# First MLP: four of twelve modulation chunks summed on TensorE in column groups

## What is computed

```python
c_act = jax.nn.silu(c)
for layer in range(DEPTH):
    mod = (c_act @ ada_w[layer] + ada_b[layer])[:, None, :]
    sh_a, sc_a, gt_a, sh_m, sc_m, gt_m = jnp.split(mod, 6, axis=-1)
    ...
    h = modulate(rms_norm(x, mlp_norm[layer]), sh_m, sc_m)
    x = x + gt_m * squared_relu_mlp(h, mlp_w1[layer], mlp_w2[layer])
    if layer == N_A_LAYERS - 1:
        kv_mod = (c_act @ kv_ada_w + kv_ada_b)[:, None, :]
```

## Time and profile before

| | us |
|---|---|
| median of 3 runs | 1641.82 |
| lowest, highest | 1637.86, 1643.93 |
| the profiled execution | 1641.37 |
| its span | 1639.5 |

### The profile page before, as it was taken

How to read it: one execution, slowest core, us unless ns; L and a number is a source line. 1 busy time by engine, 2 the same in 40 slices (tenths; PEclk the granted TensorE clock), 3 DMA queues, 4 the chain that set the end, 5 groups by cost and what they waited for, 6 DMA issues and landing times.

```text
span 1639.5 us, 21996 instructions
## 1 busy us (share of the span) xinstructions
PE 1425.1 (87%) x8482; PEld 1241.7 (76%) x8482; DVE 940.7 (57%) x1551; ACT 678.1 (41%) x1124; POOL 306.7 (19%) x257
## 2 busy tenths in 40 slices
PE   5779699999679799869999664879999898789999
PEld 1669598878679678659999554558999777579998
DVE  2777698886834554565444545446555555544443
ACT  2355444343512233334444334325444455344442
POOL 0633011010666950001001102001100100011110
PEclk9898899999778555579999776788999999889999
DMA  9877288997357220236665233027766435236651
GB/s 353 266 234 232 86 261 312 324 301 232 96 163 243 89 65 1 68 104 182 197 188 176 69 108 85 1 77 196 227 174 188 146 136 170 64 103 194 186 180 46
DMA packets 248791, 267.38 MB, mean 163 GB/s; under 512 B 10992, under 2 KB 182768, under 8 KB 248304
## 3 DMA queue, kind: packets, MB, share of 16 engines
q1 hardware_dynamic: 246064, 263.52, 51.7%
q10 hardware_dynamic: 2624, 2.47, 0.5%
HBM read 264.81 MB, written 1.15 MB: 162 GB/s over the span
## 4 chain that ended last, share of the span: by engine, by line
PE 71%; DVE 13%; issue 5%; ACT 5%; DMA 4%; POOL 1%; ACTq 0%; SPq 0%; DVEq 0%
PE bank L489 13%; PE bank L490 13%; PE bank L491 13%; PE ps_s L573 4%; PE ps_s L489 3%; PE ps_s L490 3%; PE ps_s L491 3%; PE ps_p L490 3%; PE ps_p L491 3%; PE ps_p L489 3%; DVE wlo L1103 2%; DVE acc L1122 2%; DMA wring<-in_mlp_w 2%; PE ps_p L586 2%; ACT whi L1984 2%
## 5 line engine op out<-in xcount | busy, mean ns | idle before, releaser
L1103 DVE TENSOR_TENSOR wlo<-wring,whi 128x1024 fp32r<-128x1024 f32 (+1 forms) x373 | 455.8, 1243 | 239.8 <-ACT whi L1984 235.8
L1984 ACT ACTIVATE whi<-wring 128x1024 fp32r<-128x1024 f32 (+1 forms) x373 | 388.5, 1051 | 382.3 <-PE ps_p L491 131.5
L489 PE MATMUL bank<-h_hi,whi 128*128 128x256 f32 x1216 | 352.8, 290 | 12.6 <-DVE h_lo L1197 11.2
L490 PE MATMUL bank<-h_lo,whi 128*128 128x256 f32 x1216 | 349.8, 288 | 0.0
L491 PE MATMUL bank<-h_hi,wlo 128*128 128x256 f32 x1216 | 349.3, 287 | 0.0
L489 PEld LDWEIGHTS bank<-h_hi,whi 128*128 128x128 f32 x1216 | 239.5, 197 | 18.1 <-DVE h_lo L1197 12.8
L490 PEld LDWEIGHTS bank<-h_lo,whi 128*128 128x128 f32 x1216 | 239.6, 197 | 0.7
L491 PEld LDWEIGHTS bank<-h_hi,wlo 128*128 128x128 f32 x1216 | 239.2, 197 | 0.0
L2394 POOL TENSOR_TENSOR ex<-ex 128x512 f32<-128x512 f32 x64 | 71.2, 1112 | 632.4 <-ACT g_hi L2088 632.4
L489 PE MATMUL bank<-whi,h_hi 128*128 128x512 f32 (+2 forms) x306 | 130.7, 427 | 55.3 <-DVE h_lo L1197 29.9
L491 PE MATMUL bank<-whi,h_lo 128*128 128x512 f32 (+2 forms) x306 | 127.2, 416 | 0.0
(11 more groups left out here) (306 smaller groups left out, 2213.7 us busy)
## 6 DMA issues: line engine op xcount, KB each, us to landing
wring<-in_mlp_w SPq DMA_DIRECT2D x128, 512.0 KB, 4.8
wring<-in_ada_w SPq DMA_DIRECT2D x96, 512.0 KB, 7.5
wring<-in_mlp_w_in SPq DMA_DIRECT2D x64, 512.0 KB, 4.8
wring<-in_mlp_w_out SPq DMA_DIRECT2D x64, 512.0 KB, 4.0
wring<-in_a_w_in SPq DMA_DIRECT2D x24, 512.0 KB, 5.8
wring<-in_moba_w_qkv SPq DMA_DIRECT2D x24, 512.0 KB, 4.2
wring<-in_kv_ada_w SPq DMA_DIRECT2D x16, 512.0 KB, 7.8
wring<-in_w_kv SPq DMA_DIRECT2D x12, 512.0 KB, 6.2
```

Of the source, the lines that this page charges most:

```text
L489: nc.tensor.matmul(out, lh, rh, start=first, stop=False)
L490: nc.tensor.matmul(out, lh, rl, start=False, stop=False)
L1103: v.tensor_tensor(piece_view(wlo, p), raw_view(p), piece_view(whi, p).bitcast(F32), ALU.subtract).then_inc(lo_ready, 1)
L1984: a.activation(piece_view(whi, p), raw_view(p), ACT.Copy).then_inc(hi_ready, 1)
```

## The change

Modulation chunks 2, 5, 8 and 11 of `m0` are no longer summed by DVE. PE sums their weight rows as in the opening (`row_sums`) in the ride before the one that takes their columns, that is right behind weight chunk n for modulation chunk n; ACT evicts the sums into `xn` (`rows_evict`); and in the chunk's own ride PE takes the columns from there (`row_columns`). The ring slots of these four chunks are now freed by PE, two when half of the sums are done and two at their end. `c_pad` moves from `acc` to `pos_f`, as `acc` is in use. The other chunks, the order of the loads and the drains stay.

```diff
--- before.py
+++ after.py
@@ -235,7 +235,6 @@
         pt = att[:, 2 * STRIP:].rearrange("p (b c) -> p b c", c=STRIP)
         tmp = att[:, 0:2 * W].rearrange("p (b c) -> p b c", c=W)
         acc = sb("acc", [P, 3, W])
-        c_pad = acc[:, 2, 0:KT * 32].rearrange("p (k m) -> p k m", m=32)
         early_sums = [ex[:, :, :].rearrange("p a c -> p (a c)")[:, i * W:(i + 1) * W] for i in range(3)] + [att[:, 0:W]]
         params = sb("params", [P, n_cols])
         mod = sb("mod", [P, 112])
@@ -293,6 +292,7 @@
         pos_i = extra[:, 0:T + TT].bitcast(I32)
         pos_h = extra[:, 512:512 + 2 * (T + TT)].rearrange("p (i c) -> p i c", i=2).bitcast(I32)
         pos_f = sb("pos_f", [P, 2, T + TT])
+        c_pad = pos_f[:, :, :].rearrange("p i c -> p (i c)")[:, 0:KT * 32].rearrange("p (k m) -> p k m", m=32)
         pos_q = sb("pos_q", [P, TT])
         table2 = cmp_w2[:, :, :, :].rearrange("p s i d -> p (s i d)")
         table_raw, table_rest = table2[:, 0:32], table2[:, 32:64]
@@ -392,7 +392,9 @@
 
         ada_order = [("ada0", c) for c in range(12)] + [("adakv", c) for c in range(4)] + [("ada1", c) for c in range(12)]
         opening = (2, 3, 0, 1)
-        matvec_order = [ada_order[c] for c in (4, 6, 5, 7)] + ada_order[10:22]
+        ROWS_AT = (2, 5, 8, 11)
+        on_rows = [ada_order[10 + r] for r in ROWS_AT]
+        matvec_order = [ada_order[c] for c in (4, 6, 5, 7)] + [k for k in ada_order[10:22] if k not in on_rows]
         drain_order = [ada_order[c] for c in opening + (4, 6, 5, 7, 8, 9)] + ada_order[10:]
 
         def drained_by(*chunks):
@@ -425,6 +427,33 @@
                 pe.wait_ge(matvec_done, i + 1)
                 for j in range(4):
                     last = nc.tensor.matmul(bank[:, b, j:j + 1], acc[:, i % 3, j * P:(j + 1) * P], ones[:, 0:1],
+                                            start=True, stop=True)
+                last.then_inc(filled[b], 1)
+
+            def row_sums(key):
+
+                b = bank_take(pe, ("rows", key))
+                i = on_rows.index(key)
+                for k in range(KT):
+                    load = load_of[key, k - k % 2, 0]
+                    if k % 2 == 0:
+                        load_wait(pe, load)
+                    r = 32 * (k % 4)
+                    last = nc.tensor.matmul(bank[r:r + 32, b, :], c_pad[:, k, :], loaded(load)[:, k % 2, :],
+                                            start=(k < 4), stop=(k >= 4), skip_group_check=True)
+                    if k == 3:
+                        last.then_inc(sem("row_half"), 1)
+                last.then_inc(filled[b], 1)
+                for k in range(0, KT, 2):
+                    freed[load_of[key, k, 0]] = (sem("row_half"), i + 1) if k < 4 else (
+                        filled[b], uses["rows", key][1])
+
+            def row_columns(key):
+
+                bank_emptied(pe, ("rows", key))
+                b = bank_take(pe, ("mod", key))
+                for j in range(4):
+                    last = nc.tensor.matmul(bank[:, b, j:j + 1], xn[:, 1, j * P:(j + 1) * P], ones[:, 0:1],
                                             start=True, stop=True)
                 last.then_inc(filled[b], 1)
 
@@ -684,7 +713,13 @@
 
                 def ride():
                     if ada:
-                        mod_columns(ada.pop(0))
+                        key = ada.pop(0)
+                        if key in on_rows:
+                            row_columns(key)
+                        else:
+                            mod_columns(key)
+                    if ada and ada[0] in on_rows:
+                        row_sums(ada[0])
 
                 turn_both(tag)
                 up(0)
@@ -1294,13 +1329,10 @@
                     local = p - first_piece[key]
                     if key[0].endswith("w1") and local % 2:
                         late = 2 * key[1] + local // 2
-                    if j < 4 * len(ada):
+                    if j < 4 * len(ada) and ada[j // 4] not in on_rows:
                         matvec(ada[j // 4], 2 * (j % 4), 2 * (j % 4) + 2)
                     keep_ahead("dve", min(p, base + 60))
-                    if j < 4 * len(ada):
-                        if j % 4 == 3 and j // 4 >= 2:
-                            mod_drain(ada[j // 4 - 2])
-                    if ada and j in (4 * len(ada) + 3, 4 * len(ada) + 7):
+                    if j % 4 == 3 and 0 <= j // 4 - 2 < len(ada):
                         mod_drain(ada[j // 4 - 2])
                     if other:
                         other(j)
@@ -2073,6 +2105,14 @@
                         if u >= 1:
                             copy(u - 1)
 
+            def rows_evict(r):
+
+                i = ROWS_AT.index(r)
+                src = bank_full(act, ("rows", on_rows[i]))
+                if i:
+                    bank_full(act, ("mod", on_rows[i - 1]))
+                a.activation(xn[:, 1, 0:W], src, ACT.Copy).then_inc(drained[uses["rows", on_rows[i]][0]], 1)
+
             def mlp(tag):
 
                 for b in range(2 * FF // W):
@@ -2088,6 +2128,10 @@
                     a.activation(g_hi[:, c % 2, 2 * half:2 * half + 2, :],
                                  hidden[:, b % 3, :].rearrange("p (i t) -> p i t", t=T),
                                  ACT.Square).then_inc(sem("mlp_ghi"), 1)
+                    if tag == "m0" and half:
+                        for r in (2 * c - 1, 2 * c):
+                            if r in ROWS_AT:
+                                rows_evict(r)
                 keep_ahead("act", first_piece[(f"{tag}_w2", 7)])
 
             for c in range(4):
```

## The result

The changed kernel takes 1664.6 us (median of 4 runs, 1661.1 to 1668.8) against 1641.9 (4 runs, 1637.9 to 1643.9): a ratio of 1.0143, 95% interval 1.0112 to 1.0173, or +22.8 us. The forecast was 1657.5, +16.1. The profiled execution took 1665.1 us, its span is 1663.3, 23.8 more than before's.

The account below looks back on a forecast made before the run. PE was taken as the bound, with little slack in the first MLP. Row-sums +7.7, two stands +14.0, clock +4.2 and late down chunks -9.8 sum to +16.1 us, so 1657.5 us; range 1643 to 1668.

Parts of the forecast that it names:

- The row-sums: Sums of modulation chunks 2, 5, 8, 11 on PE, all on the path: 4 x 1.92 = 7.7 us, at most 10.2.
- Late down chunks: Down chunks 6, 8, 10, 12 in the first MLP, late through DVE, lose all their lateness: -9.8 us.
- The two stands: PE idles before columns of modulation chunks 2 and 8, waiting for DVE's drains of 1 and 7: 7.0 us each.
- The timing pattern is the same: Step giving the stand before chunk 8's columns the same 7.0 us as the one before chunk 2's.
- The ring's part: Slots freed late by PE hold weight chunk 4's load to 248.7 or 249.7; by itself this delays nothing.
- The clock: PE at half clock after each of the two stands: 2.1 us each, 4.2 in all, ends 0 and 5.4.
- The two stands priced at nothing: Row-sums of 5 and 11 wait for the drains of 3 and 9; 0 us, as PE is already delayed.
- the sum with ends: The total at its low and high ends: +10.9 to +20.8 us, so 1652 to 1662.
- four stands: Rival: row-sums of 5 and 11 wait too, twice 5.2 us more; +26.5 us, 1667.9; chance 0.12.
- One after another: Side estimate: 16 row-sum passes in sequence take 3.6 us; with the 2.38x factor, four sums cost 6.1 us.
- No stand: Rival: DVE has drained chunk 1 before PE arrives at 254.5; -2.1 us, 1639.3; chance 0.10.
- short stands: Rival: weight chunk 4 lands after only 4.0 us, PE stands 3.9 us; +5.7 us, 1647.1; chance 0.14.

Follow-up runs that it names:

- E5: E1 with each of the four row-sums computed twice in a row into the same bank; 1648.4 us, ratio 1.0036 to the kernel before.
- E1: Changed kernel, but DVE drains a modulation chunk behind the first piece of weight chunk n + 3, not the last; 1643.5 us, ratio 1.0009 to before.
- E2: Kernel before, with one more bank taken at the four row-sum places (one-column matmul, 128x1 copy), no sums moved; 1662.7 us, ratio 1.0128.
- E4: Changed kernel with 28 and 35 fp32 matmuls of 128 columns filling PE's two stands; 1657.1 us, ratio 1.0097 to before.
- E8: E1 with modulation chunks 5, 7, 9 and 11 summed on PE instead of 2, 5, 8 and 11; 1640.6 us, ratio 0.9994 to before.

## Why the prediction was right, and where it was short

- **The row-sums**, forecast 7.7 us: four rows of 1.92, all on PE's path. Measured 7.7; E5 confirms that they hide behind nothing.
- **Late down chunks**, forecast -9.8: right. Down chunks 6, 8 and 12 are back at 11.8 us with columns, and 10 is held by nothing but the clock. In E1, without the stands, 1.25 of it stays. So crediting all of it was right only because PE comes late anyway, as the prediction said for 8 and 10.
- **The two stands**, forecast 2 x 7.0: the mechanism, both places and the releaser were right, as E1 and E2 show. The first was 7.4, inside its bounds, with the load 7.5 us behind half of the sums (241.90 to 249.36; forecast 6.6, at most 7.6). The second was 9.1, and the step that failed is "The timing pattern is the same". The weight load ahead of the second stand took longer to land. SP's issues in the changed kernel, ahead of the first stand and of the second:

```profile
235.28 7.67 SPq L2478 DMA_DIRECT2D wring<-in_kv_ada_w  x4
243.00 2.89 SPq L2478 DMA_DIRECT2D wring<-in_mlp_w  x4
...
319.89 5.88 SPq L2478 DMA_DIRECT2D wring<-in_mlp_w  x4
325.81 5.19 SPq L2478 DMA_DIRECT2D wring<-in_ada_w  x4
331.04 1.89 SPq L2478 DMA_DIRECT2D wring<-in_mlp_w  x4
```

Weight chunk 10, issued from 331.04, is taken up by ACT at 339.04:

```profile
339.04 1.06 ACT L2016 ACTIVATE whi<-wring 128x1024 fp32r<-128x1024 f32 x1 [6.20 <-DMA wring<-in_mlp_w]
```

That is 8.0 us after its issue, against 6.4 for chunk 4 (issued from 243.00). From half of the sums, 329.94, it is 9.1. The 12.3 us from landing to drain held both times (249.36 to 261.69, 339.04 to 351.37). What made the load 1.6 us slower is not shown. SP had issued more in the 8 us ahead of it (seven loads, four ahead of chunk 4), but in E4, with the same two groups of four ahead of it, it took 7.0.
- **The ring's part** was told with too much weight. I derived the landing from the slots that row-sums free late; but measured from the column set of chunk 1 it moved only from 8.6 to 9.3 us, 0.7 us of a stand of 7.4. The drain is late by DVE's order, and was as late before. The number came out right because the rows of before already held it.
- **The clock**, forecast 2 x 2.1: measured 3.1 and 2.7. I took a value between two gaps of another stage; here the cost was that of the longer gap (2.7 after 7.13 us idle) and above it. E4 shows that it is the clock: with it at 1.00, down chunks 4 and 10 are 0.1 us over their 11.8. A value from the nearer gap, 7.13 us, would have been 2.7 each. The low clock behind the stage was in no term.
- **Up chunk 7**, not forecast: +1.0. The banks, turned by two since chunk 5, make the second half of this up chunk wait for the drain of chunk 4. I had looked for the waits of column sets and row-sums alone. The timeline of PE:

```profile
310.43 0.39 PE L518 MATMUL bank<-h_hi,whi 128*128 128x256 f32 x1 [0.70 <-DVE mod L1171]
```

- **The two stands priced at nothing** (row-sums of 5 and 11): absent, as forecast. With the multiply-adds of all four chunks on DVE (E2) each is 1.9 us. That the missing ones of 5 and 11 alone do it, as the forecast argued, is not shown: in E8 the sums of 5 wait 0.9 us without them.
- **The sum.** By the spans the change cost 23.8 us, and the forecast was short by 7.7 (by the medians 22.8 and 6.7). Terms short by 2.5 (stands), 1.6 (clock) and 1.0 (up chunk 7) are 5.1 of it; the other 2.8, behind the stage, go with the low clock there. The result lies beyond the sum with ends, +20.8 us or 1662, and inside the stated range only because that was drawn wider, to 1668, for the sake of the four stands, which did not come.
- **One after another.** The 3.6 us for 16 passes one after another took the rate of a down chunk's split fp32r parts. An fp32 pass of 512 columns is slower, 0.43 us (last section), so that it would be 6.9, and the 6.1 us for the four sums had a wrong start. The term of 7.7 stood on the row of the opening and was not touched.
- **The rivals.** No stand and short stands fall by the timeline. Four stands falls too, though its time, 1667.9, is 3.3 us from the result and the forecast's, 1657.5, is 7.1: the time alone would have chosen the wrong mechanism.

## What to carry to other kernels

When buffers are taken in a fixed turn, an extra take shifts who waits for whom from there on: list the new pairs for all takers, and ask of each drain what stands ahead of it on its engine, since here 0.16 us of work behind 12 us of queue cost 21 us (the changed kernel against E1). Try the change with the cheap drain moved forward before judging it. Work taken off a second engine is worth only the waits that it caused on the path (9.8 of the 21.9 us by which DVE's busy time fell), while its replacement on the bottleneck costs its full length (7.7).

## What the hardware showed that I had not expected

- Sums in the four column groups: 16 fp32 passes of 512 columns take 1.92 us and, when another such group follows, 1.75 us from start to start. They run in rounds of four. PE's timeline of the changed kernel for 240.93 to 241.39, 241.82 to 242.25 and 242.25 to 242.60, each row with all passes that ran in its stretch:

```profile
240.95 0.64 PE L442 MATMUL bank<-wring,pos_f 128*32 128x512 f32 x4
...
241.40 1.04 PE L442 MATMUL bank<-wring,pos_f 128*32 128x512 f32 x8
...
241.83 1.04 PE L442 MATMUL bank<-wring,pos_f 128*32 128x512 f32 x8
```

  A round begins 0.43 us behind the one before it (241.40, 241.83), so an fp32 pass of 512 columns holds its group for 0.43 us, where a down chunk's fp32r pass takes 0.227. Plain fp32 matmuls over all 128 columns of the array agree: in the kernel before, those of 256 columns at L956 begin 0.22 us apart at full clock (eleven starts from 548.53 to 550.69). One after another the 16 would take 6.9 us, an estimate from this step, so four groups beside each other gave 3.6 times, and 3.9 back to back. The 2.38x for three groups that the Trainium skill gives (page "TensorE: Matmul & The Clock Gate", section "Measured speedup vs the span model") is less than these four gave; no run here has three.
- A stand of 7.4 us and one of 9.1 us cost 3.1 and 2.7 us more at the granted clock of 0.50, so the longer stand did not cost more. Fp32 matmuls of 128 columns on unused data kept the clock at 1.00 through the same stands (E4). Shorter waits were not safe either: behind one of 1.9 us in E2 it was 0.50.
